# Extra matmuls at three stage entries, no fills in the first attention, a plain down order and a new order of the modulation loads

## The chip, the cores and the metric

The kernel runs on one core of a Trainium2 chip. Its five engines work side by side: TensorE (PE in the profile) does matrix products and writes them to eight PSUM banks, VectorE (DVE) and ScalarE (ACT) read those and work on data in SBUF, GpSimd (POOL) does small vector work and issues some loads, SyncE (SP) issues the weight loads. Engines wait for each other by semaphores. The metric is the device time of one execution in microseconds; lower is better.

## The reference, cut to what matters

A sequence of 256 tokens with 1024 features goes through two blocks, all in float32.

```python
for i in range(2):                               # first_block
    h = rms_norm(x, mixer_norm[i])
    x = x + (dsa_mixer(h, ...) if i == 0 else rwkv7_mixer(h, ...))
    x = x + sqrelu_mlp(rms_norm(x, mlp_norm[i]), w_up[i], w_down[i])
x = rms_norm(x, final_norm)
for i in range(2):                               # second_block
    mod = silu(c) @ w_mod[i] + b_mod[i]          # 1 x 3072: shift, scale, gate
    h = rms_norm(x, g[i]) * (1 + scale) + shift
    x = x + gate * (short_conv_mixer(h, ...) if i == 0 else dilated_mixer(h, ...))
return rms_norm(x, final_g)
```

dsa_mixer is an attention over the 64 keys that an index score picks, sqrelu_mlp is `relu(h @ w_up)**2 @ w_down` with 4096 hidden features, rwkv7_mixer is a linear recurrence with its own projections (r, k, v and small "lora" products), and dilated_mixer is attention over three dilated windows.

## The kernel before

Every weight matrix streams through a ring of four slots, one granule of 128 x 1024 values (512 KB) in each. SyncE loads granule g into `raw` once the split of granule g - 4 is done. ScalarE rounds it to float32r (`w_hi`, line 737), VectorE subtracts to get the rest (`w_lo`, line 1346), and TensorE multiplies the activations, split the same way, in three terms: hi by hi, hi by lo, lo by hi. A granule gives 24 matmuls of 256 columns or 12 of 512, and the semaphore `granule_used` hands its slot back. There are 296 granules; `STREAM` names the first of each stage: dsa, dsa_out, mlp0, rkv, rwkv_out, mlp1, conv, conv_out, dil, dil_out.

The order of the work is written out by hand, one program for each engine. Three pieces matter here.

*Entering a stage.* In `entering_features` (line 2272) TensorE starts while the activations are still scaled and rounded: for each of four granules q it does eight matmuls of hi by hi, eight with the activations' rest, and eight with the weights' rest, with a wait before each. It is used for both MLPs, rkv, conv and dil. Between conv and dil (`dilated`, line 3044) TensorE turns the two token tiles by a matmul with a diagonal that holds the norm (line 2344) and, between the tiles, spreads the gate row over the partitions with two products (`mod_gate`, line 2676). VectorE adds the last conv tile, makes the diagonal (line 1355), and then scales the turned banks to `act_f` (line 1381), which ScalarE rounds (line 768).

*The MLP loops.* `step` (line 2638) computes the four up granules of one block and then the four down granules of the block before. In all steps but the first, the first down tile, six matmuls, stands before the last quarter of the last up granule (`held`, `first_tile`).

*The modulation.* `silu(c) @ w_mod` is a product of one row, done on VectorE while TensorE is in the MLPs: for each of eight k and three column blocks n, GpSimd loads a 128 x 1024 tile into `mod_w` (line 590) and VectorE multiplies and adds it (`weigh_mod`, line 1662). In the loop body VectorE takes n = 2 after the third up granule, and n = 0 and 1 at the end. GpSimd reloads a tile when `mod_used[n]` says that it was read, in the order n = 2, 0, 1, and in the first MLP issues the loads for the rwkv stage's small matrices between them, one or two per k.

In the first attention two `fill` calls (line 2658), of three and two float32 matmuls whose result nobody reads, stand before the turns of the probabilities of units 0 and 3 (line 2528).

## Time and profile before

| | us |
|---|---|
| median of three runs | 1066.7 |
| lowest, highest | 1065.21, 1069.45 |
| the profiled execution | 1065.21 |
| its span, first to last instruction | 1063.5 |
| TensorE matmuls busy | 1044.1 (98%) |
| VectorE busy | 771.0 (72%) |
| ScalarE busy | 590.0 (55%) |
| GpSimd busy | 121.0 (11%) |

In a timeline each row has the start in us from the first instruction, the duration, the engine, the line of the kernel, the operation and the tiles; rows of one kind in succession are merged, with their count behind an x, and the idle time of the engine before the row stands in brackets with what ended it. A float32 matmul shows as two records. Matmuls overlap in the pipeline: how fast they flow is read from the distance of their starts, not from their durations.

### The profile page before, as it was taken

How to read it: one execution, taken by the hardware profiler on the slowest of the kernel's cores; microseconds unless marked ns; L12 is line 12 of the kernel's file. 1: busy time of each engine (PE TensorE's matmuls, PEld its weight loads, DVE VectorE, ACT ScalarE, POOL GpSimd, SP SyncE). 2: the span in 40 equal slices, each digit the busy share in tenths (PEclk: the TensorE clock that was granted, in tenths of full speed). 3: DMA queues.
4: the chain of work that ended last, by engine and by line, in shares of the span. 5: the costliest groups of instructions: out<-in, count | busy, mean ns of one | idle time of the engine just before them, and what ended most of it. 6: DMA issues, size and time to landing. Idle time of an engine off the chain costs nothing.

```text
span 1063.5 us, 24893 instructions
## 1 busy us (share of the span) xinstructions
PE 1044.1 (98%) x10196; PEld 978.8 (92%) x10200; DVE 771.0 (72%) x1088; ACT 590.0 (55%) x900; POOL 121.0 (11%) x131
## 2 busy tenths in 40 slices
PE   9999999999999999999999999999999999999997
PEld 8966999999999789997899999999997999998885
DVE  6987666766789689768766666786676877875675
ACT  6685655555456783334555455554544667675552
POOL 0230010100000018841000000000000000000000
PEclk9999999999999999999999999999999999999999
DMA  8724688887645510002678777847654756566401
GB/s 324 243 86 138 218 286 268 272 299 273 208 123 156 162 61 4 3 5 81 217 240 292 259 244 268 279 119 235 189 178 133 218 179 212 167 215 191 141 2 39
DMA packets 83069, 192.16 MB, mean 181 GB/s; under 512 B 6000, under 2 KB 6912, under 8 KB 82992
## 3 DMA queue, kind: packets, MB, share of 16 engines
q1 hardware_dynamic: 74256, 159.93, 46.2%
q0 software_dynamic: 7584, 27.53, 7.9%
q10 hardware_dynamic: 1152, 3.59, 1.0%
q8 instruction: 59, 0.97, 0.4%
q14 instruction: 18, 0.15, 0.0%
HBM read 189.45 MB, written 1.05 MB: 179 GB/s over the span
## 4 chain that ended last, share of the span: by engine, by line
PE 89%; DVE 5%; issue 2%; ACT 2%; DMA 1%; POOL 0%; DVEq 0%; POOLq 0%; SPq 0%; ACTq 0%
PE bank L2265 13%; PE bank L2267 13%; PE bank L2266 13%; PE bank L2604 5%; PE bank L2605 5%; PE bank L2606 5%; PE bank L2279 5%; PE bank L2297 4%; PE bank L2824 4%; PE bank L2239 3%; PE bank L2241 3%; PE bank L2240 3%; PE bank L2936 1%; DMA raw<-in_dsa_w_in_dram 1%; DVE mx_d L2173 1%
## 5 line engine op out<-in xcount | busy, mean ns | idle before, releaser
L1346 DVE TENSOR_TENSOR w_lo<-raw,w_hi 128x1024 fp32r<-128x1024 f32 x295 | 357.8, 1223 | 198.1 <-ACT w_hi L737 197.6
L737 ACT ACTIVATE w_hi<-raw 128x1024 fp32r<-128x1024 f32 x295 | 309.7, 1059 | 289.8 <-PE bank L2267 143.2
L2265 PE MATMUL bank<-act_hi,w_hi 128*128 128x256 f32 x1224 | 339.2, 277 | 0.0
L2266 PE MATMUL bank<-act_lo,w_hi 128*128 128x256 f32 x1224 | 338.6, 277 | 0.0
L2267 PE MATMUL bank<-act_hi,w_lo 128*128 128x256 f32 x1224 | 338.6, 277 | 0.0
L2265 PEld LDWEIGHTS bank<-act_hi,w_hi 128*128 128x128 f32 x1224 | 229.8, 188 | 1.1 <-issue 0.7
L2266 PEld LDWEIGHTS bank<-act_lo,w_hi 128*128 128x128 f32 x1224 | 229.8, 188 | 0.0
L2267 PEld LDWEIGHTS bank<-act_hi,w_lo 128*128 128x128 f32 x1224 | 229.7, 188 | 0.0
L2604 PE MATMUL bank<-w_hi,ff_hi 128*128 128x256 f32 x512 | 141.6, 276 | 0.0
L2605 PE MATMUL bank<-w_lo,ff_hi 128*128 128x256 f32 x512 | 141.5, 276 | 0.0
L2606 PE MATMUL bank<-w_hi,ff_lo 128*128 128x256 f32 x512 | 141.5, 276 | 0.0
L2604 PEld LDWEIGHTS bank<-w_hi,ff_hi 128*128 128x128 f32 x512 | 96.2, 188 | 0.0
L2605 PEld LDWEIGHTS bank<-w_lo,ff_hi 128*128 128x128 f32 x512 | 96.1, 188 | 0.0
L2606 PEld LDWEIGHTS bank<-w_hi,ff_lo 128*128 128x128 f32 x512 | 96.1, 188 | 0.0
L2239 PE MATMUL bank<-w_hi,act_hi 128*128 128x512 f32 x168 | 67.0, 399 | 0.0
L2240 PE MATMUL bank<-w_lo,act_hi 128*128 128x512 f32 x168 | 66.4, 395 | 0.0
L2241 PE MATMUL bank<-w_hi,act_lo 128*128 128x512 f32 x168 | 66.4, 395 | 0.0
L590 POOL DMA_DIRECT2D mod_w<-in_w_mod_dram x48 | 25.8, 538 | 319.2 <-DVE mod_all L1662 239.2
L1662 DVE SCALAR_TENSOR_TENSOR mod_all<-mod_w,c_col,mod_all 128x1024 f32<-128x1024 f32 x42 | 52.4, 1276 | 0.0
L561 POOL TENSOR_TENSOR stat<-stat,half_neg 128x1 f32<-128x1 f32 x10 | 5.5, 553 | 403.6 <-DVE stat L1360 370.2
L2239 PEld LDWEIGHTS bank<-w_hi,act_hi 128*128 128x128 f32 x168 | 31.6, 188 | 8.6 <-issue 1.0
L2241 PEld LDWEIGHTS bank<-w_hi,act_lo 128*128 128x128 f32 x168 | 31.6, 188 | 7.7
(365 smaller groups left out, 1530.7 us busy)
## 6 DMA issues: line engine op xcount, KB each, us to landing
raw<-in_mlp_w_up_dram SPq DMA_DIRECT2D x64, 512.0 KB, 4.0
raw<-in_mlp_w_down_dram SPq DMA_DIRECT2D x64, 512.0 KB, 6.5
raw<-in_dil_w_in_dram SPq DMA_DIRECT2D x64, 512.0 KB, 4.3
mod_w<-in_w_mod_dram POOLq DMA_DIRECT2D x48, 512.0 KB, 6.1
raw<-in_conv_w_in_dram SPq DMA_DIRECT2D x32, 512.0 KB, 3.7
raw<-in_rwkv_w_rkv_dram SPq DMA_DIRECT2D x24, 512.0 KB, 3.8
raw<-in_dsa_w_in_dram SPq DMA_DIRECT2D x12, 512.0 KB, 7.1
raw<-in_dsa_w_o_dram SPq DMA_DIRECT2D x8, 512.0 KB, 4.3
```

Source lines behind the costliest of these rows:

```text
L737: act.activation(w_hi[:, slot, :], raw[:, slot, :], ACT.Copy).then_inc(hi_ready, 1)
L1346: dve.tensor_tensor(w_lo[:, slot, :], raw[:, slot, :], w_hi[:, slot, :].bitcast(F32), ALU.subtract).then_inc(lo_ready, 1)
L2239: pe.matmul(dst, x_hi, w_hi[:, slot, at], start=begin, stop=False, skip_group_check=True)
L2240: pe.matmul(dst, x_hi, w_lo[:, slot, at], start=False, stop=False, skip_group_check=True)
L2241: mm = pe.matmul(dst, x_lo, w_hi[:, slot, at], start=False, stop=end, skip_group_check=True)
L2265: pe.matmul(dst, w_hi[:, slot, at], hi[:, kt, :], start=begin, stop=False, skip_group_check=True)
L2266: pe.matmul(dst, w_hi[:, slot, at], lo[:, kt, :], start=False, stop=False, skip_group_check=True)
L2267: mm = pe.matmul(dst, w_lo[:, slot, at], hi[:, kt, :], start=False, stop=end, skip_group_check=True)
L2279: mm = pe.matmul(dst, w[:, slot, at], x[:, 2 * q + kk, :], start=begin and kk == 0 and f % 2 == 0, stop=end and kk == 1, skip_group_check= ...
L2604: pe.matmul(dst, x_hi, w_hi[:, at_slot, at], start=first and q == 0 and h == 0, stop=False, skip_group_check=True)
L2605: pe.matmul(dst, x_hi, w_lo[:, at_slot, at], start=False, stop=False, skip_group_check=True)
L2606: mm = pe.matmul(dst, x_lo, w_hi[:, at_slot, at], start=False, stop=last and q == PER_BLOCK - 1, skip_group_check=True)
```

## The change

It has six edits. `entering_features` can issue three extra matmuls with the operands the other way round (activations stationary, 256 columns of the weights moving), into bank 6, and does so in granule 2 of rkv, conv and dil; nobody reads the result. (`feature_granule` gets the same option, which no call uses.) Both `fill` calls of the attention go. The first down tile of each step goes back to its plain place behind the up block. In `dilated` the second gate product moves behind the second tile's turn, and on VectorE the first `w_lo` of dil moves behind the last conv tile's work. GpSimd's loads of `mod_w` wait in the order n = 0, 1, 2, and the five loads for rwkv, with the clearing of one column, stand together after k = 2.

```diff
@@ gpsimd
-                def row(k):
-                    for n in (2, 0, 1):
-                        pool.wait_ge(mod_used[n], k + done)
-                        load(n, k)
-                for k, then in enumerate(between):
-                    row(1 + k)
-                    then()
-                with pool.Fori(1 + len(between), KT) as k:
-                    row(k)
+                def columns(first, last):
+                    with pool.Fori(first, last) as k:
+                        for n in range(3):
+                            pool.wait_ge(mod_used[n], k + done)
+                            load(n, k)
+                columns(1, 3)
+                if between is not None:
+                    between()
+                columns(3, KT)
...
+            def load_lora():
+                pool.memset(R["hT"][:, :, 0:1], 0.0).then_inc(hT_edge, 1)
+                for name in ("w1", "a1", "g1"):
+                    pool.dma_start(R[name][:], ...).then_inc(lora_loaded, 16)
                 for name, rows in (("w2", slice(0, LORA)), ("a2", slice(LORA, P))):
@@ vector, conv
                 spread_rstd(3, 0)
-                split_lo(STREAM["dil"], 0)
                 add_tile("conv_out", 1, 1, 0, C["tmp"])
                 total_sum(1, 22)
                 spread_rstd(3, 1)
+                split_lo(STREAM["dil"], 0)
@@ tensor, entering_features
                 pe.wait_ge(lo_ready, g + 1)
+                if across is not None:
+                    for x, w in ((hi, w_hi), (hi, w_lo), (lo, w_hi)):
+                        pe.matmul(across[:, 0:SEQ], x[:, 2 * q, 0:P], w[:, slot, 0:SEQ], start=True, stop=True)
                 term(w_lo, hi, False, q == PER_BLOCK - 1).then_inc(granule_used, 1)
@@ tensor, first attention
-                fill(3, 5)
                 turn_probs(0)
...
-                fill(2, 5)
                 turn_probs(3)
@@ tensor, mlp
-                    feature_block(base, 4, hi, lo, (bank[0], bank[1]), it, None if first else lambda: first_tile(it, 8, 0))
+                    feature_block(base, 4, hi, lo, (bank[0], bank[1]), it)
@@ tensor, rwkv_in, conv and dilated, the calls for n == 0
+                                                  bank[6] if q == 2 else None)
@@ tensor, dilated
-                def gates():
-                    mod_gate(0)
-                    pe.wait_ge(x_updated, 22)
-                    mod_gate(1)
-                turn_scaled(3, X, LATE_TURN, gates, ordered=True)
+                turn_scaled(3, X, LATE_TURN, lambda: mod_gate(0), ordered=True)
+                mod_gate(1)
```

On GpSimd, in the first MLP's modulation, the order before is this (a row is an instruction, the semaphores it waits for in brackets; w1 is the first of the rwkv stage's matrices):

```order
L590 DMA mod_w<-in_w_mod_2_dram 128x1024 [waits mod_used2]
L590 DMA mod_w<-in_w_mod_2_dram 128x1024 [waits mod_used0]
L590 DMA mod_w<-in_w_mod_2_dram 128x1024 [waits mod_used1]
L608 DMA w1<-in_rwkv_w1_dram 128x8x64
L590 DMA mod_w<-in_w_mod_2_dram 128x1024 [waits mod_used2]
L590 DMA mod_w<-in_w_mod_2_dram 128x1024 [waits mod_used0]
L590 DMA mod_w<-in_w_mod_2_dram 128x1024 [waits mod_used1]
L608 DMA a1<-in_rwkv_a1_dram 128x8x64
```

and this with the change, from the loop over k = 1 and 2 on:

```order
L590 ISA [waits mod_used0]
L590 DMA mod_w<-in_w_mod_2_dram 128x1024
L590 ISA [waits mod_used1]
L590 DMA mod_w<-in_w_mod_2_dram 128x1024
L590 ISA [waits mod_used2]
L590 DMA mod_w<-in_w_mod_2_dram 128x1024
L597 REGISTER_ALU
L597 COMPARE_AND_BRANCH
L608 MEMSET hT 128x8
L610 DMA w1<-in_rwkv_w1_dram 128x8x64
L610 DMA a1<-in_rwkv_a1_dram 128x8x64
L610 DMA g1<-in_rwkv_g1_dram 128x8x160
```

The tile n = 2 is now reloaded after n = 0 and 1 of the same k, and the five rwkv loads follow each other.

On VectorE, at the end of conv (gated_conv is the last conv tile times its gate, per_head the diagonal), before:

```order
L1346 TENSOR_TENSOR w_lo<-raw,w_hi 128x1024
L1444 TENSOR_TENSOR gated_conv<-bank,gate 128x512
L1447 TENSOR_TENSOR X<-X,gated_conv 128x512
L1360 TENSOR_SCALAR stat<-stat 128x1
L1355 TENSOR_SCALAR per_head<-const,stat 128x128
L1381 TENSOR_SCALAR act_f<-bank,gain,mod_col 128x256 x4
```

and with the change:

```order
L1443 TENSOR_TENSOR gated_conv<-bank,gate 128x512
L1446 TENSOR_TENSOR X<-X,gated_conv 128x512
L1359 TENSOR_SCALAR stat<-stat 128x1
L1354 TENSOR_SCALAR per_head<-const,stat 128x128
L1345 TENSOR_TENSOR w_lo<-raw,w_hi 128x1024
L1380 TENSOR_SCALAR act_f<-bank,gain,mod_col 128x256 x4
```

The w_lo operation moved from before the last tile's add to between the diagonal and act_f.

On TensorE, at the same place, before (mod_all is the modulation row):

```order
L2344 MATMUL bank<-per_head,X 128x32x2x2 x8
L2676 MATMUL bank<-mod_all,const 128x512 x2
L2344 MATMUL bank<-per_head,X 128x32x2x2 x8
L2279 MATMUL bank<-act_hi,w_hi 128x256 x8
L2279 MATMUL bank<-act_lo,w_hi 128x256 x8
```

and with the change, down to the extra matmuls in granule 2:

```order
L2346 MATMUL bank<-per_head,X 128x32x2x2 x8
L2670 MATMUL bank<-mod_all,const 128x512
L2346 MATMUL bank<-per_head,X 128x32x2x2 x8
L2670 MATMUL bank<-mod_all,const 128x512
L2279 MATMUL bank<-act_hi,w_hi 128x256 x8
...
L2279 MATMUL bank<-act_lo,w_hi 128x256 x8
L2291 MATMUL bank<-w_hi,act_hi 128x256
L2291 MATMUL bank<-w_lo,act_hi 128x256
L2291 MATMUL bank<-w_hi,act_lo 128x256
L2279 MATMUL bank<-act_hi,w_lo 128x256 x8
```

One of the two gate products moved behind the second turn, and three matmuls came in before the third term of granule 2.

## Rows read from the trace of the kernel before

**Rows 1.** The page, busy time of each engine, its share and instructions

```profile
PE 1044.1 (98%) x10196; PEld 978.8 (92%) x10200; DVE 771.0 (72%) x1088; ACT 590.0 (55%) x900; POOL 121.0 (11%) x131
```

**Rows 2.** Waits of TensorE: for whom, us in total, times, longest; the largest

```profile
PE bank L3096 <- DVE p_dil L2186: 1.4, 2, 1.3
```

**Rows 3.** Timeline of TensorE in conv's entry

```profile
714.61 1.07 PE L2279 MATMUL bank<-act_hi,w_hi 128*128 128x256 f32 x8
715.51 1.07 PE L2279 MATMUL bank<-act_lo,w_hi 128*128 128x256 f32 x8
```

**Rows 4.** Timeline of the engines in rkv's entry

```profile
309.10 1.10 PE L2279 MATMUL bank<-act_hi,w_lo 128*128 128x256 f32 x8
...
310.18 1.18 PE L2279 MATMUL bank<-act_hi,w_hi 128*128 128x256 f32 x8
...
311.95 2.35 DVE L1346 TENSOR_TENSOR w_lo<-raw,w_hi 128x1024 fp32r<-128x1024 f32 x2
...
313.22 0.39 PE L2265 MATMUL bank<-act_hi,w_hi 128*128 128x256 f32 x1
```

**Rows 5.** Timeline of the engines between conv and dil

```profile
817.66 1.88 PE L2676 MATMUL bank<-mod_all,const 128*128 128x512 f32 x4
...
819.16 0.28 DVE L1355 TENSOR_SCALAR per_head<-const,stat 128x128 f32<-128x128 f32 x1 [0.66 <-POOL stat L561]
...
819.50 2.05 PE L2344 MATMUL bank<-per_head,X 128*128 128x128 f32 x16
820.32 1.90 DVE L1381 TENSOR_SCALAR act_f<-bank,gain,mod_col 128x256 f32<-128x256 f32 x4 [0.88 <-PE bank L2344]
821.35 0.63 ACT L768 ACTIVATE act_hi<-act_f 128x512 fp32r<-128x512 f32 x1 [3.10 <-DVE act_f L1381]
...
822.12 1.15 PE L2279 MATMUL bank<-act_hi,w_hi 128*128 128x256 f32 x8 [0.57 <-ACT act_hi L768]
```

**Rows 6.** Timeline of the first attention, the fills and the turns behind them

```profile
66.50 1.56 PE L2658 MATMUL bank<-const 128*128 128x256 f32 x6
...
68.59 0.63 PE L2528 MATMUL bank<-const,probs 128*128 128x128 f32 x4 [0.53 <-ACT probs L900]
...
75.81 1.13 PE L2658 MATMUL bank<-const 128*128 128x256 f32 x4
...
76.55 1.50 ACT L900 ACTIVATE probs<-probs,rden 128x128 f32<-128x128 f32 x4
...
77.36 0.63 PE L2528 MATMUL bank<-const,probs 128*128 128x128 f32 x4 [0.41 <-issue]
```

**Rows 7.** Stretches: length, PE, PEld, DVE, ACT, POOL busy, PEclk, DMA, GB/s

```profile
85.00:90.00 5.00, 3.49 (x30) 2.30 (x26) 3.72 (x8) 4.62 (x16) 0.00 (x0) 1.00 0.00 2
...
1058.00:1060.00 2.00, 0.00 (x0) 0.00 (x0) 1.27 (x3) 0.00 (x0) 0.55 (x1) 0.92 0.00 0
```

**Rows 8.** Timeline of TensorE where step 0 goes from up to down

```profile
139.44 0.28 PE L2267 MATMUL bank<-act_hi,w_lo 128*128 128x256 f32 x1
139.56 0.29 PE L2604 MATMUL bank<-w_hi,ff_hi 128*128 128x256 f32 x1
```

**Rows 9.** Timelines of GpSimd, VectorE and TensorE in one MLP step

```profile
167.28 0.53 POOL L590 DMA_DIRECT2D mod_w<-in_w_mod_dram  x1 [0.67 <-DVE mod_all L1662]
...
172.00 1.28 DVE L1662 SCALAR_TENSOR_TENSOR mod_all<-mod_w,c_col,mod_all 128x1024 f32<-128x1024 f32 x1
...
180.45 0.28 PE L2265 MATMUL bank<-act_hi,w_hi 128*128 128x256 f32 x1
```

**Rows 10.** Line 590, window 551.8 to 552.3: second and third of three loads

```profile
DMA to landing us min/median/max: 6.3/7.2/8.1
```

**Rows 11.** Line 465, window 189.5 to 190.3: a down load beside g1

```profile
DMA to landing us min/median/max: 7.7/7.7/7.7
```

**Rows 12.** The page, loads: tiles, queue, count, KB each, median us to landing

```profile
raw<-in_mlp_w_down_dram SPq DMA_DIRECT2D x64, 512.0 KB, 6.5
raw<-in_dil_w_in_dram SPq DMA_DIRECT2D x64, 512.0 KB, 4.3
```

More of the change, by code:

```diff
@@ L582, in mid_root, with modulation @@
                 pool.tensor_tensor(mid_rstd, mid_sum, half_neg[:, :], ALU.pow).then_inc(mid_rooted, 1)
-            def modulation(l, between=()):
+            def modulation(l, between=None):
                 w = A["w_mod_2"][l].rearrange("(k p) (n c) -> n k p c", p=P, c=D)
@@ L715, in _ @@
             pool.wait_ge(x_updated, 4)
-            pool.memset(R["hT"][:, :, 0:1], 0.0).then_inc(hT_edge, 1)
-            modulation(0, (load_first("w1"), load_first("a1"), load_first("g1"), load_second))
+            modulation(0, load_lora)
             roots(1)
@@ L2249, in token_granule, with feature_granule @@
                 mm.then_inc(granule_used, 1)
-            def feature_granule(g, slot, hi, lo, q, banks, groups=range(4), inc=True, held=None):
+            def feature_granule(g, slot, hi, lo, q, banks, groups=range(4), inc=True, across=None):
                 if inc:
@@ L2256, in feature_granule @@
                 for f in groups:
-                    if held is not None and f == 3:
-                        held()
                     dst = banks[f // 2][:, (f % 2) * SEQ:(f % 2 + 1) * SEQ]
@@ L2265, in feature_granule @@
                         pe.matmul(dst, w_hi[:, slot, at], hi[:, kt, :], start=begin, stop=False, skip_group_check=True)
+                        if across is not None and f == kk == 0:
+                            for x, w in ((hi, w_hi), (hi, w_lo), (lo, w_hi)):
+                                pe.matmul(across[:, 0:SEQ], x[:, kt, 0:P], w[:, slot, 0:SEQ], start=True, stop=True)
                         pe.matmul(dst, w_hi[:, slot, at], lo[:, kt, :], start=False, stop=False, skip_group_check=True)
@@ L2270, in feature_granule, with entering_features @@
                 return mm
-            def entering_features(g, slot, hi, lo, q, banks, rounded, split):
+            def entering_features(g, slot, hi, lo, q, banks, rounded, split, across=None):
                 def term(w, x, begin, end):
@@ L2288, in entering_features @@
                 pe.wait_ge(lo_ready, g + 1)
+                if across is not None:
+                    for x, w in ((hi, w_hi), (hi, w_lo), (lo, w_hi)):
+                        pe.matmul(across[:, 0:SEQ], x[:, 2 * q, 0:P], w[:, slot, 0:SEQ], start=True, stop=True)
                 term(w_lo, hi, False, q == PER_BLOCK - 1).then_inc(granule_used, 1)
@@ L2732, in rwkv_in @@
                         if n == 0:
[L2733 removed]
+                            entering_features(g, g % RING, hi, lo, q, banks, (mix_hi, q + 1), (mix_lo, q + 1), bank[6] if q == 2 else None)
                         elif c < 2:
```

20 lines of the change are left out of this document (6 added, 14 removed).

## The prediction

> **What bounds the kernel now.** I read the summary of busy time first: TensorE's matmuls fill 98% of a span of 1063.5 us [rows 1]. The table of waits, for TensorE alone, comes second: its largest total is 1.4 us [rows 2], so no wait is worth much anywhere, and an edit moves the time in three ways only: it adds or removes matmuls where TensorE runs without a gap, it lengthens one of the few hand-overs between stages, or it makes weights or activations late in a loop that runs gapless today. After that I read timelines of each place that the diff touches. The profiled execution took 1065.21 us, 1.7 us more than its span; the median of the three runs is 1066.7 and they spread over 4.2 us, so the sum below is made on 1065.21 and then laid on the median. Half a per cent, 5.3 us, is about what a measurement can tell from no change.
>
> **Nine added matmuls.** Three stages that start while their activations still arrive (rkv, conv, dil) get three extra 256-column matmuls into bank 6, between the second and the third term of granule 2. Eight such matmuls take from 714.61 to 715.51 us, a pitch of 0.113 us [rows 3]; three are 0.34 us. In conv the 12 groups of eight follow each other at that pitch, so all 0.34 is on the path. In dil too: 0.34.
>
> In rkv there is slack behind the addition. TensorE goes from the group at 309.10 to the one at 310.18 in 1.08 us instead of 0.90: the activations of granule 3 come 0.18 late. The first matmul of the next block, 313.22, stands behind the first w_lo of the pair that starts at 311.95 (2.35 us for two, so 313.13) [rows 4]. With 0.34 added the group at 309.10 starts at 309.44 and the next at 310.34 to 310.38; three groups of 0.94 later TensorE is at 313.2, and w_lo is ready there as before. Net 0 to 0.1, bounds 0 and 0.34; I take 0.05, since the hand-over at 313.22 is set by VectorE, whose order does not change there.
>
> **The hand-over from conv to dil.** Two moves. First, w_lo of dil's granule 0 was made while the last conv tile was still on TensorE; now it stands behind the second per-tile scale and in front of the four act_f operations. The scale starts at 819.16 and takes 0.28; act_f started at 820.32, when the first turned bank was full [rows 5]. Two w_lo take 2.35 us [rows 4], one at most 1.18. The moved one begins at 819.36 to 819.44 and lets act_f begin at 820.5 to 820.6, 0.2 to 0.3 late. ScalarE's rounding (821.35) and TensorE's entry (822.12, which waited 0.57 for it) follow [rows 5]. I take 0.2, since VectorE starts an operation a little before the last one ends. Second, the second gate matmul moves from before the second tile's turn to behind it. Two gates took from 817.66 to 819.50 [rows 5], 0.9 each. TensorE is then idle from 818.6 until the scale is there, starts the turn at 819.50 as before, ends it at 821.3 (16 records at 0.113) and the gate at 822.2. The entry is now due at 822.32, so the gate is covered with 0.1 to spare; without that cover it would cost at most 0.9. The raw load that waits for this w_lo on SP's queue goes out some 5 us later; the slot it fills is asked for only after TensorE has used granule 0, 2.7 us behind its entry, near 825, and such a load lands in 4.3 us [rows 12].
>
> **Five removed matmuls.** The fills stand in the first attention. Three take 1.56 us from 66.50, and the next matmul, the turn of the first probabilities, starts at 68.59 after waiting 0.53 for ScalarE. Two stand from 75.81 for 1.13, and the turn behind them starts at 77.36, when the first two of ScalarE's four scalings (76.55, 1.50 us for the four) are done, near 77.3 [rows 6]. Both turns wait for ScalarE, so removing 2.7 us of matmuls gives 0; bounds: 0 and -2.7. What is late next is the same ScalarE operation. TensorE's idle time there grows from 0.53 to 2.0 us and from 0.4 to about 1.5.
>
> That could touch the clock. In a stretch of this stage with 3.49 us of matmul in 5 the granted clock stays 1.00, that is 2.4 GHz; at the end of the program it falls to 0.5 of that (1.2 GHz), in the window 1058 to 1060, which shows 0.92 [rows 7], and by then TensorE has had nothing to do for more than 2 us. The Trainium skill (TensorE: Matmul & The Clock Gate, The HAM clock gate) says that the throttled state is the default and activity releases it; by that rule thinner activity is a risk and the fills are worth something. The trace agrees for the end of the program and shows no fall inside it.
>
> **First down tile in the MLP loops.** Before, in 12 of the loop's iterations six matmuls of the down product ran ahead of the last up group. No matmul is added or removed. Step 0 already has the plain order, and there the last up matmul starts at 139.44 and the first down matmul at 139.56, at pitch [rows 8]. I take 0. The plain order waits later for the down weights and releases the last up granule earlier, by six pitches, 0.7 us, so it can only give slack.
>
> **Order of the modulation loads.** This is the edit that can hurt. POOL loads three 512 KB tiles of mod_w (n = 0, 1, 2) per iteration of each MLP and waits before each until VectorE has read the one before it in that place. VectorE reads tile 2 in mid-iteration (172.00) and tiles 0 and 1 at its end. In the old order (2, 0, 1) tile 2 was reloaded as soon as it was free. In the new order (0, 1, 2) its load stands behind that of tile 1, which goes out at 167.28 and takes 0.53 to issue: tile 2 leaves at 167.8 and VectorE wants it at 172.00 [rows 9]. Where three such loads left together the second and third took 6.3 and 8.1 us to land [rows 10]. So it lands at 174.1 to 175.9 and VectorE stops for 2.1 to 3.9 us in each of the iterations 2 to 6 of both MLPs. Queued behind that wait are this tile's 1.28 us, the w_lo of up granule 3, then that of down granule 0 and the two ff_lo. Up granule 3 is wanted by TensorE at 180.45 [rows 9]. Its w_lo would be ready at 175.9 + 1.28 + 1.18, about 178.4: 2 us to spare. Down granule 0's follows at 179.5 and both ff_lo by 180.9; with the plain order TensorE asks for them 24 matmuls after 180.45, near 183.2. SP's load of down granule 3 leaves 4 us late, near 179, lands near 185.5 at the 6.5 us of such loads [rows 12], and TensorE asks for its product 72 matmuls after 183.2, near 191. So the stall is taken up within the iteration and costs 0.
>
> In the third iteration of the first MLP five more loads, 1.7 MB for the rwkv stage, stand behind tile 2 in one burst; before, they went one per iteration. Beside the largest of them a down load took 7.7 us [rows 11]; the burst may add 2 to 4 us to one down load. From 168.3 it would land by 180, 2.3 us before its product must be ready: 0 to 1 us, I take 0. By the Trainium skill (DMA: Bandwidth & Descriptors, Why small descriptors are slow) 256-byte pieces, which two of these loads consist of, carry some 27% overhead; an estimate by that page makes the burst about 1 us longer, still inside that room.
>
> **Sum.** 0.34 + 0.34 + 0.05 + 0.2 + 0 = 0.93 us. Profiled time 1065.21 + 0.9 = 1066.1; on the median, 1066.7 + 0.9 = 1067.6.
>
> **Rivals.**
> A, the MLP loops become bound by the late tile 2. Place: VectorE's wait for it in mid-iteration. It decides where the load takes longer than 10.1 us to land (180.45 less 1.28, 1.22 and 0.05 is 177.9, and the load leaves at 167.8), or where lateness carries over through SP's load of down granule 3. For it: 8.1 us was measured with only 1.5 MB in flight. Against: the largest landing in the rows is 2 us short of it. Beyond the point each of 10 iterations costs the excess; at 11 us 0.9 x 10 = 9 us, so 1076.
> B, the clock falls in the first attention. For it: idle stretches of 2.0 and 1.5 us come within 11 us of each other. Against: it was never below 1.00 there. If about 5 us of matmuls ran at half speed, 1067.6 + 5 = 1072.6, slower by half a per cent.
> C, the fills were on the path: a hand-over shortens and the removed 2.7 us come back, 1067.6 - 2.7 = 1064.9, still within half a per cent. Against: both turns name ScalarE, or stand where its scaling ends.
> D, the additions cost nothing because every hand-over behind them has slack: 1066.7.
>
> **How the numbers follow.** Forecast with D, whose times cannot be told apart: 0.79. A 0.08, B 0.06, C 0.07. The runs of before alone spread from 1065.2 to 1069.5, and a median of fast runs on another day can stand 1.5 us off. The range 1064.5 to 1072 holds the forecast, C, and the lower part of B and of A. Slower by over 0.5% (above 1072.0) takes A and half of B, 0.11 with rounding; faster by over 0.5% (below 1061.4) has no mechanism here, only noise or C with something unseen, 0.03; no change 0.86.
>
> **What would show it.** Nine records on the new line in front of the third terms, in bank 6; dil's first group starting 0.2 us later after the conv tile than now, with the gate right before it; VectorE's act_f there behind a w_lo. In the attention, gaps of 2.0 and 1.5 us with ScalarE as releaser and clock 1.00. In each MLP iteration VectorE waiting 2 to 4 us for mod_w, and TensorE's up and down phases still 192 pitches, 21.8 us, from one iteration to the next. Gaps on TensorE in the loops, or a granted clock below 1.00 near 70 us, would make the prediction wrong.

## The result and the profile after

The changed kernel took 1078.8 us (median of five, 1078.2 to 1081.9) beside 1069.5 us for the kernel before on the same chip (five, 1065.2 to 1071.1): a ratio of 1.011, 95% interval 1.008 to 1.014. The forecast was 1067.6 with a range to 1072.0 and 0.11 on slower; it was wrong. The profiled execution of the changed kernel lasted 1082.9 us (span 1081.2), 17.7 more than that of before, whose profiled run was the fastest of its five. All twenty runs of the changed kernel on record lie between 1075.7 and 1087.4 us. So the account below has 17.7 us to explain, of which about half is the usual difference between the kernels and the rest is how one execution differs from the next. Some 12 us of it turn out to have one cause.

The page of the changed kernel, busy time of the engines (answers to [rows 1]), then TensorE's waits, largest first (answers to [rows 2]), then VectorE's largest wait for a transfer:

```profile
PE 1057.6 (98%) x10195; PEld 991.3 (92%) x10199; DVE 768.5 (71%) x1088; ACT 590.7 (55%) x900; POOL 121.5 (11%) x131
```

```profile
PE bank L2530 <- ACT probs L899: 4.7, 3, 2.0
PE bank L2262 <- DVE w_lo L1345: 1.6, 1, 1.6
```

```profile
DVE mod_all L1661 <- DMA mod_w<-in_w_mod_dram: 52.3, 12, 5.5
```

TensorE has four matmuls more than before (nine added, five removed); it has one record less, since each of the five removed float32 matmuls shows as two. It is busy 13.5 us longer. The waits explain 1.6 us in the MLPs; the 4.7 us for the probabilities stand mostly where the fills stood. The rest is not in any table of waits; it shows only where matmuls are counted in equal stretches. Conv and dil, stretches of 40 us in which TensorE never stops, first before, then after (columns as in [rows 7]):

```profile
745.00:785.00 40.00, 40.00 (x356) 40.00 (x355) 25.25 (x27) 20.07 (x22) 0.00 (x0) 1.00 0.64 196
860.00:900.00 40.00, 40.00 (x355) 40.00 (x355) 31.59 (x38) 26.96 (x35) 0.00 (x0) 1.00 0.59 185
```

```profile
745.00:785.00 40.00, 40.00 (x342) 40.00 (x341) 25.51 (x33) 19.22 (x21) 0.00 (x0) 1.00 0.62 186
860.00:900.00 40.00, 40.00 (x342) 40.00 (x341) 31.31 (x38) 27.31 (x37) 0.00 (x0) 1.00 0.55 176
```

The same matmuls, the same granted clock of 1.00, nobody waiting: 355 in one kernel, 342 in the other (a count includes the matmuls that reach over an edge of the stretch). The starts themselves are 113.3 and 117.8 ns apart. The stream of 256-column matmuls has two pitches, and I call them fast and slow below. Where the change happens can be read off the changed kernel's conv entry, TensorE's timeline:

```profile
720.60 1.07 PE L2279 MATMUL bank<-act_hi,w_hi 128*128 128x256 f32 x8
721.51 1.07 PE L2279 MATMUL bank<-act_lo,w_hi 128*128 128x256 f32 x8
722.41 0.28 PE L2291 MATMUL bank<-w_hi,act_hi 128*128 128x256 f32 x1
722.53 0.28 PE L2291 MATMUL bank<-w_lo,act_hi 128*128 128x256 f32 x1
722.65 0.28 PE L2291 MATMUL bank<-w_hi,act_lo 128*128 128x256 f32 x1
722.77 0.99 PE L2279 MATMUL bank<-act_hi,w_lo 128*128 128x256 f32 x7
```

Groups of eight follow each other every 0.905 us up to the three added matmuls, and all of conv behind them runs at 117.8. I call a matmul that loads weights and streams activations a feature matmul, and one that loads activations and streams weights a token matmul. The added three are token matmuls among feature matmuls.

Starts of the same matmul in the two profiles, subtracted, give where 17.7 us went: 0.1 at the start; 2.7 in the first attention; 4.0 in the first MLP (1.8 around the one stop, 2.2 pitch); 2.2 in the second (pitch); 3.5 in conv (0.34 the added matmuls, 3.1 pitch); 0.2 at the hand-over; 5.2 in dil (0.34 and 4.9); rkv and the scan gave back 0.3 in this execution. Pitch is 12 us of it.

In the first attention the first matmul behind the removed fills, then two stretches (answers to [rows 6] and [rows 7]):

```profile
68.73 0.63 PE L2530 MATMUL bank<-const,probs 128*128 128x128 f32 x4 [2.02 <-ACT probs L899]
```

```profile
70.00:75.00 5.00, 4.91 (x27) 2.67 (x26) 2.95 (x9) 4.02 (x20) 0.00 (x0) 0.66 0.00 0
80.00:85.00 5.00, 5.00 (x27) 3.04 (x28) 4.73 (x11) 4.31 (x14) 0.00 (x0) 0.66 0.31 105
```

The turns wait for ScalarE, 2.0 and 1.8 us (forecast 2.0 and 1.5), and behind each wait the granted clock is 0.66: part of the stretch ran at 1.2 GHz. The Trainium skill (TensorE: Matmul & The Clock Gate, The HAM clock gate) has the throttled state as the default that activity releases; by that rule the fills were worth something, and here the trace agrees.

The modulation tile and the one stop of TensorE, in the iteration after the burst of rwkv loads: VectorE, then TensorE.

```profile
205.11 1.28 DVE L1661 SCALAR_TENSOR_TENSOR mod_all<-mod_w,c_col,mod_all 128x1024 f32<-128x1024 f32 x1 [5.35 <-DMA mod_w<-in_w_mod_dram]
206.31 2.35 DVE L1345 TENSOR_TENSOR w_lo<-raw,w_hi 128x1024 fp32r<-128x1024 f32 x2
```

```profile
207.58 0.39 PE L2262 MATMUL bank<-act_hi,w_hi 128*128 128x256 f32 x1 [1.55 <-DVE w_lo L1345]
```

The tile landed in 7.4 us, which is not long. It left late. ScalarE, VectorE and GpSimd ahead of it:

```profile
191.64 1.06 ACT L736 ACTIVATE w_hi<-raw 128x1024 fp32r<-128x1024 f32 x1 [4.80 <-DMA raw<-in_mlp_w_down_dram]
```

```profile
192.74 1.22 DVE L1345 TENSOR_TENSOR w_lo<-raw,w_hi 128x1024 fp32r<-128x1024 f32 x1 [4.64 <-ACT w_hi L736]
```

```profile
197.02 1.11 POOL L590 DMA_DIRECT2D mod_w<-in_w_mod_dram  x2 [0.63 <-DVE mod_all L1661]
```

The late tile 2 of the iteration before (read at 180.61 after a wait of 5.41 us) held up a w_lo, so SyncE's load of down granule 3 left at 183.2 and took 8.3 us. ScalarE and VectorE waited for it, VectorE read tiles 0 and 1 late, and tile 2 left at 197.6, 27.3 us behind the one before it (170.3) and 8.3 us ahead of the hour at which its w_lo was wanted (205.9).

### The profile page after: what moved, and what is told of

It is laid out like the page before. It is cut to its first block, busy times and chain, and to the rows that moved or that the text cites. A ratio compares the mean times of both kernels' runs of the same rounds, so it can differ in the third digit from the quotient of the medians.

```text
span 1081.2 us, 24917 instructions
## 1 busy us (share of the span) xinstructions
PE 1057.6 (98%) x10195; PEld 991.3 (92%) x10199; DVE 768.5 (71%) x1088; ACT 590.7 (55%) x900; POOL 121.5 (11%) x131
## 4 chain that ended last, share of the span: by engine, by line
PE 84%; DVE 7%; DMA 4%; issue 2%; ACT 2%; DVEq 0%; POOL 0%; SPq 0%; POOLq 0%; ACTq 0%
PE bank L2262 12%; PE bank L2266 12%; PE bank L2267 12%; PE bank L2605 5%; PE bank L2604 5%; PE bank L2606 5%; PE bank L2279 4%; PE bank L2300 4%; PE bank L2818 3%; PE bank L2238 3%; PE bank L2240 3%; PE bank L2239 3%; DMA mod_w<-in_w_mod_dram 2%; PE bank L2930 1%; DVE w_lo L1345 1%
## 5 line engine op out<-in xcount | busy, mean ns | idle before, releaser
L1661 DVE SCALAR_TENSOR_TENSOR mod_all<-mod_w,c_col,mod_all 128x1024 f32<-128x1024 f32 x42 | 52.5, 1281 | 52.3 <-DMA mod_w<-in_w_mod_dram 52.3
```

Of the source, the lines that this page charges most:

```text
L1661: dve.scalar_tensor_tensor(total, part, c, total, ALU.mult, ALU.add).then_inc(mod_used[n], 1)
```

## The experiments

Eighteen kernels ran, in five groups; each group has its own runs of before, 136 in all. "Profile" is the shift of the last out-projection's matmuls against the kernel before's profile. First the four parts of the change, each alone.

**The nine matmuls alone** (a_across):

```
 (before) + across in rkv, conv and dil, as in the change
```

> The kernel before with only the nine added matmuls (three each in rkv, conv and dil), nothing else changed. Theory 1, a pitch that toggles: a run of 256-column matmuls goes at one of two pitches, 113.3 or 117.8 ns, and changes to the other one where TensorE turns from products that load weights and stream activations to products that load activations and stream weights; the added matmuls are of the second kind, so conv and dil behind them go at 117.8 if they went at 113.3 ahead of them: 0.34 + 3.1 us in conv, 0.34 + 4.9 us in dil, rkv within 1 us: 8 to 9.5 us slower than before, and the MLP loops as before. Rival 1: the added matmuls cost their own time only, 9 x 0.113 = 1.0 us, and the slower conv and dil of the changed kernel come from another of its parts. Rival 2, the slower pitch is a matter of the execution and not of the code: conv and dil are as likely fast as slow in this one.

Ratio 1.0031 (1.0008 to 1.0055), median 1070.3. Conv as theory 1 had it, but dil not: it was entered slow, and the three matmuls made it fast. TensorE's timeline in dil:

```profile
832.73 1.10 PE L2279 MATMUL bank<-act_hi,w_hi 128*128 128x256 f32 x8
833.67 1.10 PE L2279 MATMUL bank<-act_lo,w_hi 128*128 128x256 f32 x8
834.61 0.28 PE L2293 MATMUL bank<-w_hi,act_hi 128*128 128x256 f32 x1
...
834.97 1.07 PE L2279 MATMUL bank<-act_hi,w_lo 128*128 128x256 f32 x8
835.87 1.07 PE L2279 MATMUL bank<-act_hi,w_hi 128*128 128x256 f32 x8
```

0.94 us from group to group ahead, 0.90 behind. So the same three matmuls slow one stage and speed the other: they toggle. Profile +5.5, of which conv is 3.5 and dil 0.6. The other 1.3 us stand ahead of the first attention, where nothing was edited. My 8 to 9.5 assumed that dil was entered fast; rival 1, 1.0 us, is out, and rival 2 holds for dil's entry alone: that is a matter of the execution, as the groups of runs further down show.

**The loads' order and the burst** (a_mod), **the order alone** (b_order), **the burst alone** (b_burst), **tile 2 second** (d_mid):

```
-                    for n in (2, 0, 1):
+                    for n in (0, 1, 2):    # a_mod, b_order;  d_mid: (0, 2, 1)
 a_mod, b_burst: the five rwkv loads in one burst, as in the change
```

> The kernel before with only the order of the modulation loads (0, 1, 2) and the five rwkv loads in one burst. Theory: VectorE waits up to 5.5 us for tile 2 in each iteration, TensorE waits in one iteration only, the one after the burst, 1.6 us; no other loss: 1 to 2.5 us slower than before, pitches in the MLP loops as before (six held matmuls and the last up group at 117.8, the rest at 113.3). Rival: the late tile 2 or the denser loads are also what slows the matmuls of every second iteration: 5 to 6.5 us slower, and the pitch of 117.8 in every second iteration of both MLPs.

> The kernel before with the modulation loads in the order 0, 1, 2 and nothing else: the rwkv loads stay one to an iteration. Theory: VectorE waits for tile 2 in mid-iteration, 2 to 6 us each time, TensorE nowhere: same time as before within 1 us. Rival: in the iterations with an rwkv load between, tile 2 lands past 10.1 us and TensorE waits 1 to 3 us in one to three of them, after which the pitch may have changed for the rest of the loop (2 to 3 us more).

> The kernel before with the five rwkv loads in one burst behind the third iteration's modulation loads and nothing else: the order stays 2, 0, 1. Theory 1: tile 2 goes first and VectorE never waits for it, so the burst alone delays only the down loads; TensorE waits under 1 us: within 1 us of before. Rival 1: the burst is the whole harm: landings of 10 to 15 us for the down weights, TensorE waits 3 to 6 us in the iteration behind it, and 12 us in all with the pitch changed after the wait. Rival 2: the two edits hurt only together, this one and the order's alone within 1 us.

> The kernel before with the modulation loads in the order 0, 2, 1: tile 2 goes out second of three, not third, nothing else changed. Theory: a second load landed in 6 to 8 us, VectorE wants tile 2 some 4.5 us after it goes out, so it waits 2 to 4 us instead of up to 6 and TensorE never waits for a w_lo; no stretch of the MLP loops changes its pitch and the time is that of before within 0.2%. Rival: any order that makes VectorE wait in mid-iteration costs what the changed order costs, 0.6% to 1%.

Ratios: a_mod 1.012 (1.008 to 1.016), b_order 1.0097 (1.0071 to 1.0122), b_burst 0.9998 (0.9975 to 1.0022), d_mid 1.0002 (0.998 to 1.0024). The order alone costs nearly what the whole change costs, the burst alone nothing, and tile 2 in second place nothing: VectorE's wait for it falls from 54.0 us to this row's 13.5.

```profile
DVE mod_all L1662 <- DMA mod_w<-in_w_mod_dram: 13.5, 11, 2.5
```

In b_order's profile no wait of TensorE for w_lo is large enough to be listed. Two starts are late all the same, at 246.2 and at 651.8. Around the second stands this: VectorE and TensorE, then counts ahead and behind.

```profile
649.32 1.28 DVE L1662 SCALAR_TENSOR_TENSOR mod_all<-mod_w,c_col,mod_all 128x1024 f32<-128x1024 f32 x1 [6.04 <-DMA mod_w<-in_w_mod_dram]
650.52 2.35 DVE L1346 TENSOR_TENSOR w_lo<-raw,w_hi 128x1024 fp32r<-128x1024 f32 x2
```

```profile
651.52 0.28 PE L2267 MATMUL bank<-act_hi,w_lo 128*128 128x256 f32 x1
651.79 0.39 PE L2265 MATMUL bank<-act_hi,w_hi 128*128 128x256 f32 x1
652.01 0.28 PE L2266 MATMUL bank<-act_lo,w_hi 128*128 128x256 f32 x1
```

```profile
622.00:642.00 20.00, 20.00 (x178) 20.00 (x177) 13.01 (x12) 11.15 (x14) 1.59 (x3) 1.00 0.76 265
657.00:675.00 18.00, 18.00 (x155) 18.00 (x154) 12.03 (x12) 9.31 (x13) 1.58 (x3) 1.00 0.80 286
```

The w_lo behind the late tile came about 0.15 us late; the next two starts are 0.27 and 0.22 apart instead of 0.11. The stop itself costs 0.27 us, the one at 246.2 cost 0.2. But the pitch is fast up to the late start and slow from the next one on, with no turn of operands between, and so are conv and dil: +1.9 us in the second MLP, +3.4 in conv and +5.1 in dil, profile +10.0. 20 us hold 178 matmuls ahead, so 18 us would hold 160; behind it they hold 155. The profiled run of b_order was the fastest of its four (1075.2; the others 1078.5 to 1084.0), and what the others lost beyond it was not traced.

In a_mod the stops are longer: 3.6 us at once and, with the shorter ones, 4.4 us in all, beside my 1.6. Behind the long one the granted clock is 0.60 from 208 to 212 us, which costs another 1.6 us. Its profile is +18.2 us: 9.3 in the first MLP, 0.9 in the second, 3.4 in conv and 5.1 in dil. So the rival, which had a slower pitch in the loops, was nearer than my theory, and too small as well. My expectation for b_order, no stop and no loss, was wrong; so was rival 2 of b_burst. b_burst's and d_mid's profiles (+5.0, +5.2) differ from before's in dil's pitch alone.

**The MLP order alone** (a_held):

```
-  feature_block(..., None if first else lambda: first_tile(it, 8, 0))
+  feature_block(..., None)
...                                  # and down() issues all its tiles
```

> The kernel before with the plain order in the MLP steps: the first down tile no longer runs ahead of the last up group; same matmuls, other order. Theory 1, the toggling pitch: with the first down tile ahead there are two changes to products that stream weights in each iteration, so the pitch comes back; in the plain order there is one, so every second iteration goes at 117.8 ns instead of 113.3: 192 x 4.5 ns = 0.87 us in each of about 3 of 6 iterations a loop, less the six to twelve matmuls per iteration that go at 117.8 before; 2 to 2.5 us in each MLP, 4 to 5 us slower in all, with no new wait on TensorE. Rival 1: the order makes no difference to the pitch, within 0.5 us of before, and the alternation in the changed kernel comes from the loads. Rival 2: the plain order waits for something, which would show as a gap on TensorE at the step from up to down.

Ratio 1.0038 (1.0013 to 1.0064), profile +4.4: 2.2 in each MLP, with no new wait. Stretches of 20 us in three consecutive iterations:

```profile
142.00:162.00 20.00, 20.00 (x179) 20.00 (x179) 13.88 (x14) 10.14 (x13) 3.02 (x5) 1.00 0.90 315
164.00:184.00 20.00, 20.00 (x172) 20.00 (x171) 13.49 (x13) 9.84 (x12) 2.49 (x4) 1.00 0.84 279
186.00:206.00 20.00, 20.00 (x179) 20.00 (x178) 14.10 (x13) 10.47 (x14) 2.49 (x4) 1.00 0.89 306
```

Fast, slow, fast, and so on to the end of both loops: in the plain order each iteration turns once from feature to token matmuls, with the held tile twice. Theory 1 holds in its number.

**The fills alone** (a_fills):

```
-                fill(3, 5)
-                fill(2, 5)
```

> The kernel before without its five fill matmuls in the first attention, nothing else changed. Theory: TensorE's idle time there grows to about 2.0 and 1.7 us, the granted clock falls to about 0.66 in two stretches near 70 and 80 us, and the attention ends 2.5 to 3 us later: 2 to 3 us slower. Rival 1: the clock fell in the changed kernel by chance or through another of its parts; without fills alone it stays 1.00 and the time is that of before within 0.5 us. Rival 2: the fills were on the path, 2.7 us faster.

Ratio 1.0035 (1.0014 to 1.0056). In the attention the profile shows one fall of the clock instead of two, worth 1.3 us:

```profile
65.00:75.00 10.00, 7.80 (x48) 4.44 (x46) 8.06 (x22) 7.81 (x35) 0.00 (x0) 0.83 0.00 0
75.00:85.00 10.00, 8.31 (x57) 4.49 (x56) 9.86 (x23) 9.98 (x34) 0.00 (x0) 1.00 0.15 54
```

The three profiles without fills (this one, the changed kernel, c_back) lost 1.3, 2.7 and 2.7 us there; the 17 with fills show 1.00 there. So the theory holds in kind, and in size at the low end. But idle time does not settle alone when the clock falls. In a_fills' profile it fell once more, near the end of dil, where nothing was edited:

```profile
1030.00:1035.00 5.00, 4.10 (x21) 3.91 (x21) 0.88 (x3) 1.38 (x4) 0.00 (x0) 0.67 0.00 0
```

TensorE was busy 2.98 of the 5 us ahead of it, with no idle stretch over 0.5 us; the kernel before has the same 2.98 of 5 there and kept 1.00. This second fall costs 1.2 us. The median rose by 4.4 us; which of the runs had which falls, and how dil was entered in each, was not traced.

**What toggles** (b_kinds, b_twice, c_set). Extra matmuls of a chosen kind stand ahead of a granule's third term:

```
+  for _ in range(count):            # held_ is loaded, moved is streamed
+      ...
+      pe.matmul(bank[6][:, 0:SEQ], held_[:, 0:P], moved[:, 0:SEQ], start=True, stop=True)
```

> The kernel before with small groups of extra 256-column matmuls into bank 6, ahead of the third term of a granule, to see which kind changes the pitch of what follows. In conv: granule 1 three that load weights and stream activations (the kind around them), granule 2 one that loads activations and streams weights, granule 3 two of that second kind. In dil: granule 1 three that load and stream activations, granule 2 three that load and stream weights, granule 3 four of the second kind. Theory 1, the pitch toggles at each change to matmuls that load activations and stream weights, however many they are: conv at 113.3 ns up to the single one in granule 2, 117.8 from there to granule 3, 113.3 again behind the two, which leaves conv fast; dil changes at granule 3 and at no more than one of granules 1 and 2 (whichever operand it is that counts), and entering fast it ends at 117.8 after one change and at 113.3 after two. Rival 1, a count: only an odd number of extra matmuls changes the pitch: conv changes at granules 1 and 2 and not at 3; dil at 1 and 2 and not at 3. Rival 2, no toggle: any interruption sets the pitch to 117.8 for good: conv is slow from granule 1 on.

> The kernel before with three added matmuls (activations loaded, weights streamed) at two places each of conv and dil, granules 1 and 2; rkv as before. Theory 1, the toggle: the second three undo what the first three did, so with twice the matmuls conv and dil are faster than with three: 2 x 0.68 us of added matmuls and at most 0.2 us for the stretches of 24 matmuls between them, 1.5 us over before, where three alone cost 3.5 in conv. Should dil be entered at 117.8, it is so again behind both, 5.4 us over before. Rival, each addition only costs more: conv and dil both at 117.8 behind granule 1, 9 us over before.

> The kernel before with two 512-column matmuls (activations loaded, weights streamed) in granule 2 of conv and of dil, and three 256-column ones of that kind in granule 3. Idea under test: both MLPs are entered right behind 512-column matmuls, and always at 117.8; if such matmuls set the slow pitch whatever it was before, the three behind them set the fast one, and conv and dil go at 113.3 in every execution: all runs within 2 us of one another, at 1.8 us over the fastest of before. Rival 1: the 512-column matmuls toggle as the others do; two changes leave each stage at the pitch at which it was entered, and the runs spread over 6 us as those of before do. Rival 2: they do not count, and one change inverts what was entered: mostly slow conv, 4 us over before.

b_kinds, TensorE in conv:

```profile
712.02 0.50 PE L2294 MATMUL bank<-act_hi,w_hi 128*128 128x256 f32 x3
712.36 1.07 PE L2279 MATMUL bank<-act_hi,w_lo 128*128 128x256 f32 x8
...
715.08 0.28 PE L2294 MATMUL bank<-w_hi,act_hi 128*128 128x256 f32 x1
715.20 1.10 PE L2279 MATMUL bank<-act_hi,w_lo 128*128 128x256 f32 x8
...
718.02 0.40 PE L2294 MATMUL bank<-w_hi,act_hi 128*128 128x256 f32 x2
718.26 1.11 PE L2279 MATMUL bank<-act_hi,w_lo 128*128 128x256 f32 x8
```

Three extra feature matmuls change nothing; one token matmul makes it slow; the two at 718.02 leave it slow, against theory 1, and against the count rival (three feature matmuls did nothing). b_twice went to slow and back in conv and, entered slow, needed both groups in dil to become fast (1.0007, 0.9990 to 1.0024). Counted over all twenty profiles, where no stop is near: a turn from feature to token matmuls took fast to slow in 238 of 238 cases and slow to fast in 321 of 360. So there is an exception; the slow pitch may have two forms, one of which needs a turn more, which is a guess. In dil b_kinds' three groups brought all eight runs to within 1.3 us (1070.5 to 1071.7; 1.0012, 0.9996 to 1.0027), which led to d_ww. c_set's 512-column matmuls did not fix the entry: 1.0004 (0.9983 to 1.0026), and its runs still fall into two groups (1067.2 to 1069.3, 1072.1 to 1073.7). Rival 1: in conv two of them took the stream from fast to slow and the three of 256 columns took it back, so token matmuls of 512 columns toggle too.

**Do stops toggle?** (c_gaps, e_stops): TensorE signals GpSimd and waits for its answer, 12 times ahead of a third term, 24 times ahead of a first or second.

> The kernel before with twelve small stops of TensorE in conv, one in each of twelve granules of 24 matmuls (a signal to GpSimd and back, 0.2 to 0.6 us each), nothing else added. Theory 1: such a stop by itself can change the pitch of what follows, so of the twelve stretches of 24 matmuls between the stops some go at 113.3 ns and some at 117.8. Rival: a stop costs its own length and nothing more; every stretch goes at the pitch at which conv was entered.

> The kernel before with 24 small stops of TensorE in conv, one to a granule: twelve ahead of a first term (weights and activations both rounded), twelve ahead of a second term (the same weights with the rest of the activations), four lengths of 0 to 0.4 us each, nothing else added. Theory: a stop at such a place can leave what follows at the other pitch, as behind the late weights of the changed order, so some stretches of 24 matmuls go at 117.8 ns. Rival: as with the stops ahead of third terms all stay at 113.3, and a stop alone does not do it.

One of e_stops' stops:

```profile
721.99 0.28 PE L2273 MATMUL bank<-act_hi,w_lo 128*128 128x256 f32 x1
722.37 0.38 PE L2273 MATMUL bank<-act_hi,w_hi 128*128 128x256 f32 x1
722.59 0.28 PE L2273 MATMUL bank<-act_lo,w_hi 128*128 128x256 f32 x1
```

All 36 stops left the stream fast (rival 1 in both; 1.0035, 1.0009 to 1.0062, and 1.0088, 1.0054 to 1.0122, the stops' own length for the most part: 3.8 and 7.6 us in conv; e_stops' profile has 5.1 more in dil, entered slow). A stop costs its length and 0.11 us for the first start behind it (0.22 instead of 0.11). Stops by a late w_lo are another matter. In the three profiles with the new order five of them caught the stream fast. The starts were 1.83 us apart at 205.8 in the changed kernel, 0.22 at 246.0 and 0.27 at 651.5 in b_order, 0.41 at 194.9 (at a turn back to feature matmuls) and 0.22 at 181.0 in a_mod. Behind the first four the pitch is slow from the next start on, behind the last it stayed fast. Waits of 0.26 to 0.36 us at rkv's entry did the same as the four in the changed kernel, c_back and c_entry; in c_entry, c_set and e_stops a wait of 0.26 us there took slow to fast. So such stops can change the pitch, and neither their length nor their place ahead of a first term decides it: e_stops has 0.265 us ahead of a first term, and the stream stayed fast. The made stops come back a fixed time after TensorE's own signal, with start distances repeated to 1 ns (0.151, 0.265, 0.378, 0.492 us); the late w_lo comes at any time. Whether that is the difference was not settled.

**One line put back** (c_back), the changed kernel with the order 2, 0, 1:

> The changed kernel with one line put back: the modulation loads in the order 2, 0, 1 again; the burst of rwkv loads, the plain order in the MLP steps, the missing fills and the nine added matmuls stay. Theory 1: the order's late tile 2 opens small gaps on TensorE, and each gap can leave the stream at the slower pitch until something changes it back; with the order put back the gaps go, and what is left is the alternation in the MLPs (4.4 us), conv at 117.8 behind its three added matmuls (3.5), dil either way, and up to 2.8 for the clock in the first attention: 1074 to 1080 with a median near 1076, 2 to 4 us below the changed kernel. Rival: the order accounts for all of the change, and this kernel is within 0.3% of before.

Ratio 1.0066 (1.0042 to 1.0091), median 1076.3: theory 1 as written. The order is worth 2.5 us here by the medians, 2.7 by the profiles and 4.8 by the ratios, whose intervals overlap. That is less than it costs alone, since the other parts toggle too.

**Buying the pitch back** (c_entry, d_entry3, d_one, d_ww, e_both):

```
 MLP, first up block, granule 1:   + 1 (c_entry) or 3 (d_entry3, e_both) token matmuls
 MLP, step 0:                      + first_tile ahead of the last up group
 dil:  d_one  granules 1, 2, 3:    + 1, 3, 3 token matmuls
       d_ww, e_both  granule 2:    + 3 that load and stream weights;  granule 3: + 3 token
```

> The kernel before with one added matmul (activations loaded, weights streamed) in granule 1 of each MLP's first up block, and with the first down tile ahead of the last up group in the first step too, as in all later steps: the first 200 matmuls of each MLP, which all profiles so far show at 117.8 ns, then go at 113.3. Theory 1: 2 x (0.9 less 0.12 less 0.05) = 1.4 us less than before, if the pitch behind the first step is the fast one as before; should it come out slow, the loops run at 117.8, 5 us more in each. Rival, the pitch there is set by the stage and not by what went ahead: no gain, 0.2 us more.

> The kernel before with three added matmuls in granule 1 of each MLP's first up block (one did not change the pitch there), and the first down tile ahead of the last up group in the first step as in the later ones. Theory: three do change it, so some 150 matmuls of each MLP go at 113.3 instead of 117.8: 0.7 us less 0.34 for the three and 0.1 for the held tile, 0.3 us gained in each MLP, and the loops as fast as before. Rival: the loops then run at 117.8, 3 to 5 us slower in each.

> The kernel before with added matmuls in dil only (activations loaded, weights streamed): one in granule 1, three in granule 2, three in granule 3. So far three such took 113.3 to 117.8, and 117.8 to 113.3 except behind a single one or a stop; if there are three conditions (fast; slow, back to fast at the next change; slow, one change away from the former), one and three and three bring the first two to fast: all runs in one group near 1067, 1 us over the fast runs of before, or in two groups still if dil is entered in the third. Rival: the two groups of before have nothing to do with dil's pitch: the same two groups, each 1 us later.

> The kernel before with added matmuls in dil only: three that load and stream weights in granule 2, three that load activations and stream weights in granule 3. In the kernel that had both (with four instead of three, and three more of a third kind ahead) all eight runs fell within 1.3 us. Theory: this pair brings dil to 113.3 whichever way it is entered, and the runs form one group near 1066.5. Rival: it inverts or keeps what was entered, and there are two groups 4 to 5 us apart.

> The kernel before with three added matmuls in each MLP's first up block and the first down tile held in its first step too (about 0.4 us gained in each MLP so far), and in dil three matmuls that load and stream weights and three that load activations and stream weights (1 us, and every run in the fast group so far). Theory: the two add up and all runs lie between 1065 and 1067.5, the median at 1066, faster than before by 0.2 to 0.4% as before's own median stands between its two groups. Rival: the shift in the MLPs changes how dil is entered in a way that the pair does not mend, and a second group appears near 1071.

c_entry missed: one matmul left the entry slow and nothing was gained (0.9986, 0.9965 to 1.0007). d_entry3's three made it fast, 0.3 us in the first MLP's profile and 0.3 in the second, but its median does not show it (0.9992, 0.9972 to 1.0012): seven of its twelve runs lie above 1069.5, five below 1065.4. How dil is entered is left to chance. d_one and d_ww take that chance away. d_ww's dil, entered slow in its profile:

```profile
829.24 1.10 PE L2279 MATMUL bank<-act_lo,w_hi 128*128 128x256 f32 x8
830.18 0.51 PE L2294 MATMUL bank<-w_hi 128*128 128x256 f32 x3
830.53 1.10 PE L2279 MATMUL bank<-act_hi,w_lo 128*128 128x256 f32 x8
...
833.36 0.52 PE L2294 MATMUL bank<-w_hi,act_hi 128*128 128x256 f32 x3
833.71 1.07 PE L2279 MATMUL bank<-act_hi,w_lo 128*128 128x256 f32 x8
```

The 136 runs of before lie in two groups with nothing between: 66 from 1064.3 to 1067.5 and 70 from 1069.3 to 1072.6, their medians, 1065.6 and 1070.5, 4.9 us apart, which is what the slow pitch costs in dil (45 granules of 24 matmuls at 4.5 ns). The kernel before has one profile, fast in dil. That its groups are dil's pitch rests on their distance, on the profiles of b_burst, d_mid and c_entry, which are slow in dil alone or nearly so, and on what follows. All 12 of d_one (1066.2 to 1068.6), all 12 of d_ww (1066.0 to 1067.8) and all 12 of e_both (1064.8 to 1067.6) are in one group. Ratios: d_one 0.9985 (0.9970 to 1.0001), d_ww 0.9982 (0.9966 to 0.9998), e_both 0.9988 (0.9971 to 1.0005), the last beside runs of before of which 11 of 19 were in the lower group. So d_ww beats before by 0.2%, the interval just clear of 1; e_both has the lowest median of all, 1065.9, but its interval holds 1.

## Why the prediction was wrong

- **"An edit moves the time in three ways only".** This is the step that failed. There is a fourth: an edit of the order in which feature and token matmuls follow each other sets the pitch of what stands behind it, 4% on over half of the kernel; a small delay can change it too. Of the 17.7 us this is 12. It was in the profile of before, unread: a group of eight in [rows 4] is 1.10 us long, those in [rows 3] 1.07, and the prediction itself counts groups of 0.94 us in rkv and eight matmuls in 0.90 in conv.
- **Nine matmuls, 0.73 us.** Their own time was right, 0.34 each in conv and dil. What they do to the pitch was not a term: +3.1 in conv, and in dil up to 4.9 less or 4.9 more by how it is entered. In rkv 0.05 was forecast and a_across has 0.08; there the added three found the slow pitch and left it slow, which the prediction could not know.
- **Hand-over, 0.2.** The changed order cost 0.17: the scale is at 831.38, w_lo behind it, act_f 1.33 us later instead of 1.16 [rows 5]. Right.

```profile
831.38 0.29 DVE L1354 TENSOR_SCALAR per_head<-const,stat 128x128 f32<-128x128 f32 x1 [0.66 <-POOL stat L561]
831.58 1.22 DVE L1345 TENSOR_TENSOR w_lo<-raw,w_hi 128x1024 fp32r<-128x1024 f32 x1
...
832.71 0.99 DVE L1380 TENSOR_SCALAR act_f<-bank,gain,mod_col 128x256 f32<-128x256 f32 x2
```

- **Fills, 0.** The cover was read rightly, the idle 2.0 and 1.8 us came nearly as written (2.0 and 1.5), and the clock, held at rival B's 0.06, fell in all three profiles without fills. Price 1.3 to 2.7 us, not 5. The argument against B, "never below 1.00 there", was taken from a kernel with fills.
- **Held tile, 0.** No wait came, and it cost 4.4 us through the pitch. "It can only give slack" looked at waits alone.
- **Order of the loads, 0; rival A at 10.1 us.** VectorE waited longer than the 2.1 to 3.9 us forecast: 52.3 us in 12 waits, the longest 5.5. That "the stall is taken up within the iteration" failed. SyncE's load of down granule 3, forecast to leave near 179 and land near 185.5, left at 183.2 and landed at 191.5, and tile 2 of the next iteration left with 8.3 us to its hour instead of 12.65. That is A's second condition, lateness carried over through this load, and it made the changed kernel's one stop of 1.8 us. Landings reached 10.1 us beside the burst and 9.7 without it; in b_order tile 2 left 12.2 us ahead of its hour, 0.4 less than assumed, and was late by about 0.15. A's price of the stops alone was small, 0.5 us in b_order, 1.8 in the changed kernel, 4.4 in a_mod; b_order's loss came with the pitch behind it.
- **The range.** Its upper end rested on the spread of before's runs, 1065.2 to 1069.5, read as noise. It is two values of one kernel, and an edit can move a kernel from one to the other.

The Trainium skill (TensorE: Matmul & The Clock Gate, Back-to-back issue gap) gives 262 cycles at 2.4 GHz as the gap of 256-column matmuls taken by themselves; an estimate by that figure is 109 ns. The traces differ: they show 113.3 and 117.8 ns in a stream with weight loads, and the difference between the two decided this case.

## What to carry to other kernels

Before costing an edit in a kernel bound by TensorE, count matmuls in equal stretches of each stage: two counts for one kind of matmul mean that there is a pitch to win or lose, and no table of waits shows it. When runs of one kernel fall into two groups, find the stage that differs before calling it noise. A tile that lands late behind slack is not free if its w_lo can come even 0.15 us late, and a filler that hides nothing may be holding the clock.

## What was not expected of the hardware

- Two pitches of 256-column matmuls at granted clock 1.00, 113.3 and 117.8 ns, each kept for up to 130 us (dil) without a change; the start of each weight load against its matmul is nearly the same in both, 2 to 4 ns behind, so the trace does not say what differs.
- Which operand is loaded and which is streamed toggles the pitch on the way from feature to token matmuls, and seldom on the way back (477 of 498 turns kept it). Token matmuls of 512 columns do it too (c_set). Why is open; other addresses were not tried.
- A late operand can toggle it as well: behind four of five late w_lo that met a fast stream it was slow, behind 36 made stops of up to 0.4 us never.
- Clock: with TensorE idle 2.0 us ahead of it, a stretch of 5 us at 0.66 of the full clock; with the fills, idle 0.5, none in 17 profiles. Yet one profile fell to 0.67 at 1030 to 1035 us with no idle stretch over 0.5 us ahead of it, where the kernel before, as busy, kept 1.00.
